# Delta-rule side chain on GpSimd, gate-sum rows read directly, norms by ones products, two weight quarters in one load

## The reference

```python
xn = rmsnorm(h, norm_w)
proj = xn @ w_in          # u_pool, z_pool, q, k, v, z_dn, b, a, gate_pool, gate_dn
y_pool = causal_multiscale_pool(u_pool, pool_mix, pool_scale) * silu(z_pool)
q = l2norm(heads(silu(conv4(q)))) * HD ** -0.5      # k too; v is only convolved
lmat = strict_lower(k_beta @ k.T * exp(gcum_i - gcum_j))   # per chunk of a head
tmat = inv(eye + lmat)
# per chunk: v_new = tmat @ (v_beta - k_beta * exp(gcum) @ S); o = q_dec @ S + qk @ v_new
#            S = S * g_last + k_dec.T @ v_new
y_dn = rmsnorm(o, dn_norm_w) * silu(z_dn)
merged = sigmoid(gate_pool) * (y_pool @ w_pool_out) + sigmoid(gate_dn) * (y_dn @ w_dn_out)
out = rmsnorm(h + merged @ w_o, final_norm_w)[:, N_META:]
```

## Time and profile before

| | us |
|---|---|
| runs before (3) | 2039.75, 2041.04, 2042.32; median 2041.04 |
| the profiled execution | 2038.36 |
| its span, first to last instruction | 2036.8 |
| PE busy | 1862.6 (91%), 15073 instructions |
| DVE busy | 1435.5 (70%) |
| ACT busy | 953.8 (47%) |
| POOL busy | 70.3 (3%) |
| mean granted clock of PE | 0.968 |

### The profile page before, as it was taken

The page is one execution under the profiler, slowest core; times in us unless marked ns, Lnnn a source line. Parts: engine busy times, 40 slices in busy tenths (PEclk is TensorE's granted clock), DMA queues, the critical chain, the costliest instruction groups (busy, mean ns, idle before and its releaser), DMA issues.

```text
span 2036.8 us, 40992 instructions
## 1 busy us (share of the span) xinstructions
PE 1862.6 (91%) x15073; PEld 1741.3 (85%) x15073; DVE 1435.5 (70%) x2628; ACT 953.8 (47%) x2148; POOL 70.3 (3%) x94
## 2 busy tenths in 40 slices
PE   5899999898988989888898898999997899999998
PEld 4889999888887888878888898899997688888886
DVE  7867799878778788787887878677776544335332
ACT  5544446455454554545555456455555322224222
POOL 2000010000000000000000000000000000000000
PEclk8999999899999999999999899999998999999999
DMA  5334355443454434544444355354546443437312
GB/s 151 84 83 110 108 152 163 115 138 99 121 150 113 147 97 113 151 112 148 108 112 151 101 152 135 88 144 128 141 124 217 145 136 122 153 107 260 125 37 83
DMA packets 355651, 260.93 MB, mean 128 GB/s; under 512 B 36865, under 2 KB 315866, under 8 KB 354794
## 3 DMA queue, kind: packets, MB, share of 16 engines
q1 hardware_dynamic: 283954, 197.35, 33.4%
q10 hardware_dynamic: 65160, 39.94, 6.8%
q0 software_dynamic: 6336, 21.08, 3.0%
HBM read 216.82 MB, written 42.60 MB: 127 GB/s over the span
## 4 chain that ended last, share of the span: by engine, by line
PE 62%; DVE 16%; issue 9%; DMA 6%; ACT 4%; ACTq 2%; DVEq 1%; SPq 0%; POOLq 0%; POOL 0%
PE pj L701 34%; PE pj L666 16%; PE pg L666 9%; DVE wl L1475 4%; PE pt L666 3%; DMA branch_scratch<-tm 2%; DVE stg L1796 2%; ACT wh L1026 2%; DMA tm<-gate_sum_scratch 2%; DMA yraw<-branch_scratch 1%; DVE st L1855 1%; DVE st L1858 1%; DVE raw L1508 1%; DVE raw L1499 1%; PE pt L832 1%
## 5 line engine op out<-in xcount | busy, mean ns | idle before, releaser
L701 PE MATMUL pj<-xh,wh 128*128 128x256 f32 (+2 forms) x3136 | 936.1, 299 | 92.9 <-DVE wl L1475 42.4
L701 PE MATMUL pj<-xl,wh 128*128 128x256 f32 (+2 forms) x3136 | 903.0, 288 | 0.0
L701 PE MATMUL pj<-xh,wl 128*128 128x256 f32 (+2 forms) x3136 | 901.6, 288 | 0.0
L1026 ACT ACTIVATE wh<-raw 128x512 fp32r<-128x512 f32 x784 | 484.9, 629 | 605.8 <-PE pj L701 423.7
L701 PEld LDWEIGHTS pj<-xh,wh 128*128 128x128 f32 x3136 | 611.1, 195 | 112.4 <-issue 54.0
L1475 DVE TENSOR_TENSOR wl<-raw,wh 128x512 fp32r<-128x512 f32 x784 | 534.8, 687 | 193.4 <-ACT wh L1026 187.6
L701 PEld LDWEIGHTS pj<-xl,wh 128*128 128x128 f32 x3136 | 612.6, 195 | 1.0 <-issue 1.0
L701 PEld LDWEIGHTS pj<-xh,wl 128*128 128x128 f32 x3136 | 609.9, 194 | 0.0
L666 PE MATMUL pj<-yh,bwh 128*128 128x512 f32 x384 | 149.8, 390 | 1.4 <-DVE yl L2010 1.4
L666 PE MATMUL pj<-yl,bwh 128*128 128x512 f32 x384 | 149.4, 389 | 0.0
L666 PE MATMUL pj<-yh,bwl 128*128 128x512 f32 x384 | 149.4, 389 | 0.0
(11 more groups left out here) (284 smaller groups left out, 1986.0 us busy)
## 6 DMA issues: line engine op xcount, KB each, us to landing
raw<-in_w_in SPq DMA_DIRECT2D x224, 512.0 KB, 4.1
head_scratch<-stg ACTq DMA_DIRECT2D x64, 264.0 KB, 2.8
rawb<-in_w_dn_out SPq DMA_DIRECT2D x16, 1024.0 KB, 6.2
rawb<-in_w_o SPq DMA_DIRECT2D x12, 1024.0 KB, 5.2
kq<-head_scratch SPq DMA_DIRECT2D x8, 1056.0 KB, 8.4
gates_scratch<-stg ACTq DMA_DIRECT2D x32, 256.0 KB, 3.5
rawb<-in_w_pool_out SPq DMA_DIRECT2D x8, 1024.0 KB, 5.2
yraw<-branch_scratch SPq DMA_DIRECT2D x1, 5120.0 KB, 20.6
```

Of the source, the lines that this page charges most:

```text
L701: mm = pe.matmul(bank[:, c0:TH], w[:, slot, k, :], xx[what][:, kt, c0:TH], start=opens and one and kt == 0, stop=closes and last and kt == ...
L1026: return act.activation(dst, src, ACT.Copy)
```

## The change

The inversion and all its DMAs go from DVE's hooks and ACT's queue to GpSimd (`inversion`), as one sequence behind `mk_ready`. The next pair's row differences are loaded straight into `dec` and made on GpSimd behind the inversion, once the last product that reads `qk` (the same memory) is done; y's store (`head_out`) is issued behind them. The squared norms of k and q come from ACT's squares of whole tiles (into `st` and `mk`) and 18 products with a column of ones into free columns of `pg[2]`; the transposes of q, their squares, the gram diagonals and their reductions go. RA and RC are loaded by one DMA of 1 MB with runs of 1 KB once both are free, and `s2` of the next block runs at t = 9 rather than at t = 0. The 20 tiles of `yraw` are loaded in five parts with the block loads of gate blocks 6 to 10. The loops on SP and GpSimd over gate blocks and pairs are written out.

```diff
-SLOT_OF = {1: 0, 2: 1, 3: 1, 4: 3, 5: 3, 6: 4, 7: 4, NEXT: 4}
-RA, RB, RC, RF, RE = range(5)
+SLOT_OF = {1: 0, 2: 2, 3: 2, 4: 3, 5: 3, 6: 4, 7: 4, NEXT: 4}
+RA, RC, RB, RF, RE = range(5)
...
+        squares_of = [t[:, :].rearrange("p (h t) -> p h t", h=2) for t in (st, mk)]
...
+        raw_ac = raw[:, 0:2, :, :].rearrange("p s k c -> p (s k c)").rearrange("p (k c) -> p k c", c=CW)
+
+        def weights(which):
+
+            return raw_ac[:, :, P * which:P * (which + 1)] if which in (RA, RC) else raw[:, which, :, :]
...
...
+        ALL_TOK = 2 * SLOTS + 4
...
+            def load_ac(col):
+                sp.dma_start(raw_ac, w_in[0, 0:KH * P, bass.ds(col, CW)].rearrange("(k p) c -> p k c", p=P)
+                             ).then_inc(raw_loaded[RA], 16)
...
-                sp.wait_ge(dec_diff, d + 1)
+                need(sp, y_stored, 16 * d)
...
                 sp.wait_ge(lo_done, base + after(order, 1))
-                load_raw(RA, col)
                 sp.wait_ge(sum_done, 4 * b + 3)
-                load_raw(RC, col)
+                load_ac(col)
...
-            with sp.Fori(2, NGATE // 2) as i:
-                for k in range(2):
-                    block_loads(CP_GATE0 + 2 * i + k - 1, COL_GATE + i * (2 * CW) + k * CW)
-
-
-            sp.wait_ge(y_stored, 16 * PAIRS)
-            sp.wait_ge(yp_stored, 16 * GROUPS)
             y_rows = y_d.rearrange("(k p) t -> p k t", p=P)
-            sp.dma_start(yraw[:, 0:20, :], y_rows[:, 0:20, :]).then_inc(yraw_loaded, 16)
+            for i in range(4, NGATE):
+                block_loads(CP_GATE0 + i - 1, COL_GATE + i * CW)
+                if i == 6:
+                    sp.wait_ge(y_stored, 16 * PAIRS)
+                    sp.wait_ge(yp_stored, 16 * GROUPS)
+                if 6 <= i < 11:
+                    part = slice(4 * (i - 6), 4 * (i - 5))
+                    sp.dma_start(yraw[:, part, :], y_rows[:, part, :]).then_inc(yraw_loaded, 16)
...
+                    if h == 1:
+                        wait(norm_square, 2, 2)
+                        for at in range(NSLOT):
+                            cols = tokens(at % NCH) if at < SLOTS else slice(0, C)
+                            mm = product(pg[2][:, 64 + at:65 + at], squares_of[0][:, at // NCH if at < SLOTS else at - SLOTS, cols], one, True, True)
+                        for at in range(SLOTS):
+                            mm = product(pg[2][:, 64 + NSLOT + at:65 + NSLOT + at], squares_of[1][:, at // NCH, tokens(at % NCH)], one, True, True)
+                        mm.then_inc(norm_mm, 1)
...
+                if m < 2:
+                    if m == 0:
+                        wait(kq_loaded, 16, 16)
+                        wait(tr_mm, NCH, 0)
+                    else:
+                        wait(o_tr, 2, 0)
+                    act.activation(squares_of[m], kq[:, m, :, :], ACT.Square).then_inc(norm_square, 1)
...
...
-                if m == F0 + 2:
-                    wait(mk_ready, 1, 1)
-                    act.dma_start(full_rows(gram_d), slots(mk)).then_inc(mk_stored, 16)
-                    act.dma_start(blocks(gram_d, NBLK - 2, NBLK).rearrange("a j c -> j a c"), tail(mk)).then_inc(mk_stored, 16)
+                    wait(norm_mm, 1, 1)
+                    act.activation(rk[:, 0, :], pg[2][:, 64:64 + NSLOT], ACT.Sqrt, bias=eps).then_inc(norm_sqrt, 1)
+                    act.activation(norms[:, 1, 0:SLOTS], pg[2][:, 64 + NSLOT:64 + NSLOT + SLOTS], ACT.Copy).then_inc(norm_kept, 1)
...
-                            act.activation(src, src, ACT.Square, accum_out=norms[:, 1, at:at + 1]).then_inc(tok_done, 1)
...
-                if m == F0 + 6:
-                    wait(mk_stored, 32, 32)
-                    act.dma_start(gblk, blocks(gram_d, 0, NBLK)).then_inc(blk_loaded, 16)
-                if m == W0 + 5:
-                    wait(w_turned, 1, 1)
-                    act.wait_ge(blk_zeroed, 32)
-                    for scratch, block_of in zip(inv_d, (wblk, wtr)):
-                        act.dma_start(blocks(scratch, 0, NBLK), block_of).then_inc(w_stored, 16)
...
-                dve.wait_ge(raw_loaded[RC], 16 * b + 16)
+                dve.wait_ge(raw_loaded[RA], 16 * b + 16)
...
-                    if t == (3 if first else 0):
+                    if first and t == 3:
...
+                    if not last and t == (14 if first else 9):
+                        s2(b + 1)
...
-                if G0 <= m < G0 + 2:
-
-                    h = m - G0
-                    wait(gram_mm, 2, h + 1)
-                    tt(head(st, h), pg[h][:, :].rearrange("p (n c) -> p n c", c=C), ident.unsqueeze(1).broadcast_to([P, NCH, C]),
-                       ALU.mult).then_inc(gram_diag, 1)
-                    if h == 1:
...
-                        dve.tensor_reduce(norms[:, 0, 0:SLOTS], slots(st), AX_X, ALU.add)
-                        dve.tensor_reduce(norms[0:META, 0, SLOTS:], tail(st), AX_X, ALU.add).then_inc(norm_sum, 1)
...
                 if m == F0:
                     wait(decay_exp, 1, 1)
+                    wait(norm_mm, 1, 1)
                     for h in range(2):
                         tt(head(mk, h), pg[h][:, :].rearrange("p (n c) -> p n c", c=C), head(dec, h), ALU.mult).then_inc(mq_ready, 1)
+                    wait(norm_kept, 1, 1)
...
-                if m == W0:
-
-                    wait(blk_loaded, 16, 16)
-                    dve.tensor_scalar(wblk, gblk, -1.0, None, ALU.mult).then_inc(w_init, 1)
-                    wait(w_init, 2, 1)
-                    dve.memset(wblk.rearrange("p a i -> p (a i)")[:, 0:BS * BS:BS + 1], 1.0).then_inc(w_init, 1)
-                    wait(w_init, 2, 2)
-                if W0 <= m and 1 + NSTEP * (m - W0) < BS - 1:
...
-                    if j == BS - 2:
-                        wait(w_step, BS - 2, BS - 2)
-                        dve.tensor_copy(wtr, wblk.rearrange("p a i -> p i a")).then_inc(w_turned, 1)
...
+            def row_differences(d):
+
+                need(pool, qkv_mm, NCH * d)
+                pool.dma_start(dec[:, 0:XC], g_d[d:d + 1, 0:SLOTS, :].rearrange("a i c -> a (i c)").broadcast_to([P, XC])
+                               ).then_inc(rowg_loaded, 16)
+                pool.dma_start(tail(dec), g_d[d:d + 1, SLOTS:, 0:META].broadcast_to([META, 2, META])).then_inc(rowg_loaded, 16)
+                pool.wait_ge(rowg_loaded, 32 * d + 32)
+                own = table[:, d, GCUM, :]
+                pool.tensor_tensor(slots(dec), slots(dec), bc(own[:, 0:SLOTS], C), ALU.subtract)
+                pool.tensor_tensor(tail(dec), tail(dec), bc(own[0:META, SLOTS:], META), ALU.subtract).then_inc(dec_diff, 1)
+
+            def inversion(d):
+
+                pool.wait_ge(mk_ready, d + 1)
+                pool.dma_start(full_rows(gram_d), slots(mk)).then_inc(mk_stored, 16)
+                pool.dma_start(blocks(gram_d, NBLK - 2, NBLK).rearrange("a j c -> j a c"), tail(mk)).then_inc(mk_stored, 16)
+                pool.wait_ge(mk_stored, 32 * d + 32)
+                pool.wait_ge(norm_mm, d + 1)
+                pool.dma_start(gblk, blocks(gram_d, 0, NBLK)).then_inc(blk_loaded, 16)
+                pool.wait_ge(blk_loaded, 16 * d + 16)
+                pool.tensor_scalar(wblk, gblk, -1.0, None, ALU.mult).then_inc(w_init, 1)
+                pool.wait_ge(w_init, 2 * d + 1)
+                pool.memset(wblk.rearrange("p a i -> p (a i)")[:, 0:BS * BS:BS + 1], 1.0).then_inc(w_init, 1)
+                pool.wait_ge(w_init, 2 * d + 2)
+                done = (BS - 2) * d
+                for j in range(1, BS - 1):
+                    rest = BS - 1 - j
+                    own = tblk[:, 0:j * rest].rearrange("p (a i) -> p a i", a=j)
+                    if j > 1:
+                        pool.wait_ge(w_step, done + j - 1)
+                    pool.tensor_tensor(own, wblk[:, 0:j, j:j + 1].broadcast_to([NBLK, j, rest]),
+                                       gblk[:, j:j + 1, j + 1:BS].broadcast_to([NBLK, j, rest]), ALU.mult).then_inc(w_prod, 1)
+                    pool.wait_ge(w_prod, done + j)
+                    pool.tensor_tensor(wblk[:, 0:j, j + 1:BS], wblk[:, 0:j, j + 1:BS], own, ALU.subtract).then_inc(w_step, 1)
+                pool.wait_ge(w_step, done + BS - 2)
+                pool.tensor_copy(wtr, wblk.rearrange("p a i -> p i a")).then_inc(w_turned, 1)
+                pool.wait_ge(w_turned, d + 1)
+                pool.wait_ge(blk_zeroed, 32)
+                for scratch, block_of in zip(inv_d, (wblk, wtr)):
+                    pool.dma_start(blocks(scratch, 0, NBLK), block_of).then_inc(w_stored, 16)
+                pool.wait_ge(w_stored, 32 * d + 32)
+                pool.wait_ge(tok_done, ALL_TOK * (d + 1))
+                pool.dma_start(slots(tm), full_rows(inv_d[1])).then_inc(tm_loaded, 16)
+                pool.dma_start(slots(st), full_rows(inv_d[0])).then_inc(st_loaded, 16)
+                pool.dma_start(tail(st), blocks(inv_d[0], NBLK - 2, NBLK).rearrange("a j c -> j a c")).then_inc(st_loaded, 16)
+
```

(25 more changed lines are left out.)

62 lines of the change are left out of this document (18 added, 44 removed).

## The result

| | before | after |
|---|---|---|
| median of the runs, us | 2041.68 (4 runs) | 2108.23 (2106.16 to 2112.19, 4 runs) |
| ratio, 95% interval | | 1.0329 [1.0311, 1.0347] |
| span of the profiled execution, us | 2036.8 | 2105.9 |
| granted clock | 0.968 | 0.954 |

What follows compares the result with a forecast made beforehand. TensorE was taken as the bound, with GpSimd's chain deciding when it starts L0 in each of eight rounds. 2038.4 - 2 (rounds) - 3 (pooling blocks) - 15.5 (yraw) = 2018, plus 2.7 for the median: 2021 us, range 1957 to 2075.

Steps and rivals of the forecast that it cites:

- part 3: Inversion on GpSimd: chain from ready mk to landed tm 39.3 us (31 to 46), a gain of 0.3 us a round.
- S + 60.3: Forecast start of delta step L0's first triangular product, 60.3 us after block k's start S; before, S + 61.65 in one round.
- Part 1: Work taken off TensorE, VectorE and ScalarE ahead of L0: TensorE could be there some 10 us sooner.
- (a): In a round, the eight q transposes, their squares and the wait go: 3.8 us a round.
- Part 2: Ones products for the norms ahead of the k transposes: 3 us, mk ready at S + 21, today 19.6.
- B: The forecast itself: chains of 36 to 42 us, 1992 to 2045 us; chance 0.45.
- C: Slower rival: each GpSimd step waits for VectorE, issues cost 1.5 us more, chain 46 us: 2075 us; chance 0.25.
- Part 4: Row differences at the round's end, directly into dec: 0 to 1 us a round, hidden by the 3.98 us gap.
- Part 5: Weight loads: joint load and earlier s2 cost nothing; relieved block heads take some 3 us out of the pooling blocks.
- rival D: Loads: S2 or S3 waits for its load where VectorE catches up, 1 us in 32 pair blocks: 2050 us; chance 0.05.
- Part 6: yraw in five loads during gate blocks 6 to 10: gain of 15.5 us, between 13 and 18.
- A: Faster rival: the chain hides at 31 us, L0 at S + 53, 60 us gained in all: 1963 us; chance 0.22.

Runs made afterwards that it cites:

- a_head: The changed kernel with s2 run again at the head of its block (t = 0), not at t = 9 of the block before: 2080.8 us, 1.0180 of before.
- b_inv: b_two with the whole inversion on GpSimd, DMAs and operations, and nothing else of the change: 2032.5 us, 0.9954 of before.
- b_two_ones: b_two with the norms by ones products; q transposes, their squares and gram diagonals gone: 2045.4 us, 1.0019 of before.
- b_two: The kernel before with RA and RC in one load and yraw loaded in five parts: 2018.4 us, 0.9862 of before.
- inv_half: b_inv with only the first 7 of the 14 rank-one steps, the other half of the inversion left out: 1954.1 us, 0.9558 of before.
- b_rows: b_two with the row differences loaded directly into dec at the round's end: 2030.3 us, 0.9947 of before.
- b_late: The kernel before with only s2 of the next block moved to t = 9: 2066.4 us, 1.0114 of before.
- b_ac: The kernel before with only RA and RC joined in one load of 1 MB: 2033.4 us, 0.9942 of before.

## Why the prediction was wrong

**The step that failed.** It is the sum of part 3, "L0 then comes at S + 60.3", a gain of 0.3 us a round, with nothing charged behind L0. Measured are S + 64.7 in the mean (63.4 to 65.8), 4.0 us later than before, and 4.1 us more from L0 to the next S: 65 us in eight rounds in place of a gain of 2. Ahead of L0 two terms were too small: mk was ready at S + 22.1 to 23.3 (the sum has 21), and the chain took 39.7 to 43.1 us, 41.8 in the mean (39.3). Behind L0 three terms stood at nothing or next to it: the early `s2`, the row differences, and the clock behind the wait (a_head, which lacks the early `s2`, still takes 68.6 us there; b_inv, which lacks the row differences and the ones products as well, 67.1; before 65.6). Outside the rounds the early `s2` lost 17 us where the sum has a gain of 3.

**Part 1, right and wrong.** TensorE would be at L0 some 10 us sooner: in b_inv it stands there 8.1 to 9.2 us ahead of tm, so the relief of VectorE and ScalarE is real. (a) is wrong: the q transposes' 3.8 us gave nothing in b_two_ones, since VectorE sets block q's pace. The wait's name was the squares; the one that was late next was `wl`.

**Part 2, wrong.** The size was near (4.0 to 4.4 us against 3), the place of it in the sum was not. I let the products delay mk alone, by 1.4 us against the kernel before; from b_two to b_two_ones mk came some 5 us later, and where L0 doesn't wait for tm, as in b_two_ones, the 4 us are TensorE's own, in every round, not beside anything: +27 us in place of nothing. In the changed kernel TensorE waits for tm at L0, so there its own 4 us are covered and mk's delay is what counts. No run takes the products alone out of it; a_head, which has them and the direct row differences, is 48 us above b_inv, which has neither.

**Part 3, right in the mechanism, short in the sum.** The steps took 18.5 to 19.1 us in seven of the rounds (16.7 in the last), and 20.7 with the three other operations in the round shown, against 18.5 for all 31. GpSimd's large issues were 0.9 to 1.06 us and not 1.8, five of them 4.0 us less than my 9; the landings and the handovers took that back, 22.0 us for all DMA pieces against 20.8. Chain 40 to 43 us against 39.3: some 3 us, between B and C. I also had a late microsecond at one. In the round shown 4.6 us of clock lie behind the 8.00 us of wait, but other waits further on take up part of that: b_inv comes to L0 8.2 us later than inv_half (S + 59.6 against S + 51.4 in the mean) and takes 1.1 us more behind it, so the price is 1.1 to 1.2 there. And the kernel before had 3 to 4 us of slack at the old mk; with mk later by the ones products and the chain longer, both were spent.

**The trade that I missed.** I took the inversion as one thing. Its DMAs on GpSimd are worth 19 to 28 us, its operations there cost 33 to 42.

**Part 4, wrong.** I put the 2.29 us operation's effect at 0 to 1 us "hidden by the 3.98 us". It is 12 us in all (b_rows), 1.5 a round ahead of S: VectorE's lateness in block z falls on TensorE before the gap begins, and the gap doesn't shrink by it. The gap never covered this operation: it ran behind S.

**Part 5, wrong twice.** The joint load wasn't nothing but -10 us. And s2 waited for RF: three splits behind step 6 take 2.6 us and not 3 x 1.43, because VectorE catches up there after two sums, while the load takes 4. This was rival D, by its mechanism (VectorE catching up) and its price of 1 us a block (0.9 in gate blocks, 1.4 over the five blocks with pair 0's), at a chance of 0.05. It should have had far more. The 3 us out of the pooling blocks came with `s2` alone (228.4 to 226.0 us in b_late), but not with the joint load (229.7 in b_ac, 230.2 in the changed kernel).

**Part 6, right.** -15.0 us in the changed kernel, -14 alone, against -15.5.

**The rivals.** C came nearest: TensorE waits for tm in every round, 2075 us. With the 27 us of D's kind on it, it gives 2102, but that is partly luck. C's chain of 46 us with issues 1.5 us dearer than ScalarE's did not come (43 at most, issues 0.5 us dearer for the loads of 512 KB), and L0's lateness is worth 32 of the 66 us; ones products and row differences, which C doesn't have, make up for the rest. I had let the rivals exclude one another. A put 60 us on a hidden chain; inv_half, with half of the steps left out, lies 64 us under b_two. So that price was near, and that the chain wasn't hidden was the error. That A's 1963 is near inv_half's 1954 is chance, since inv_half has neither the ones products nor the row differences nor the early `s2`.

The parts measured alone sum up to -24 + 14 + 27 + 12 + 25 = +54 us (the inversion on GpSimd as a whole 14, s2 as the mean of 27 and 23). The change lost 66. Of the remaining 12 us 9 stand between b_inv and a_head: ones products and row differences cost 48 us there and 39 on b_two. That mk's delay meets the longer chain there, which no single part has, is my guess for them; no run shows it.

## What to carry to other kernels

A stall's name is not its cause: before a wait is counted as gain, ask which engine would be late there next, and run the kernel with that edit alone. Move the DMAs of a side chain and its arithmetic in two steps: an idle engine's queue was a gain here, its arithmetic beside a busy VectorE took 0.62 us an operation in place of 0.24 and made the chain too long to hide. A load may be consumed earlier only by as much as the consumer's shortest time from the issue allows, not its mean pace.
